# A block triangular inverse on TensorE: 64 by 64 products for 128 by 128 ones, and two weight-split steps at other places

## The reference

```
a_mat = where(strict, (k_beta @ k.T) * decay, 0)
sol   = triangular_solve(a_mat + I, rhs, lower=True, unit_diagonal=True)
u, w  = sol[..., :dv], sol[..., dv:]
```

## Time and profile before

| | us |
|---|---|
| median of 3 runs | 945.17 |
| the profiled execution | 945.2 |
| its span in the trace | 943.3 |
| TensorE matmuls busy | 921.9 (98%) |
| VectorE busy | 610.8 (65%) |
| ScalarE busy | 497.4 (53%) |
| GpSimd busy | 31.1 (3%) |

### The profile page before, as it was taken

The page is one execution under the profiler, slowest core; times in us unless marked ns, Lnnn a source line. Parts: engine busy times, 40 slices in busy tenths (PEclk is TensorE's granted clock), DMA queues, the critical chain, the costliest instruction groups (busy, mean ns, idle before and its releaser), DMA issues.

```text
span 943.3 us, 13998 instructions
## 1 busy us (share of the span) xinstructions
PE 921.9 (98%) x5274; PEld 784.3 (83%) x5274; DVE 610.8 (65%) x1039; ACT 497.4 (53%) x868; POOL 31.1 (3%) x43
## 2 busy tenths in 40 slices
PE   8999989999999999899999999999999999999998
PEld 6999889799989898767888888888876788888887
DVE  6787966776565687778655555556887665555443
ACT  5478441473565566566544444545576654444432
POOL 2001000000000012100000000010000000000000
PEclk9999999999999999999999999999999999999999
DMA  9545231366444545214555655555434365555560
GB/s 331 180 135 159 92 97 46 122 210 212 149 134 136 183 154 192 90 45 134 179 178 180 192 190 191 182 181 180 142 128 133 92 197 192 188 178 178 180 200 22
DMA packets 106293, 148.22 MB, mean 157 GB/s; under 512 B 12564, under 2 KB 59344, under 8 KB 106112
## 3 DMA queue, kind: packets, MB, share of 16 engines
q1 hardware_dynamic: 102014, 145.34, 47.5%
q0 software_dynamic: 704, 1.77, 0.5%
q10 hardware_dynamic: 3522, 0.39, 0.3%
HBM read 146.03 MB, written 1.45 MB: 156 GB/s over the span
## 4 chain that ended last, share of the span: by engine, by line
PE 87%; DVE 7%; ACT 4%; issue 1%; DMA 1%; ACTq 0%; SPq 0%; DVEq 0%
PE ps L1889 25%; PE ps L1891 25%; PE ps L1890 24%; PE ps L1989 4%; DVE wlo L1162 3%; ACT whi L642 1%; PE ps L2135 1%; PE ps L2129 1%; DMA raw<-in_a_w_in 1%; PE ps L2283 1%; DVE G L1334 1%; PE ps L2491 0%; PE ps L2522 0%; PE ps L2070 0%; PE ps L2089 0%
## 5 line engine op out<-in xcount | busy, mean ns | idle before, releaser
L1162 DVE TENSOR_TENSOR wlo<-raw,whi 128x1024 fp32r<-128x1024 f32 (+1 forms) x271 | 320.3, 1223 | 210.9 <-ACT whi L642 210.6
L642 ACT ACTIVATE whi<-raw 128x1024 fp32r<-128x1024 f32 (+1 forms) x271 | 270.2, 1045 | 269.1 <-PE ps L1891 269.0
L1889 PE MATMUL ps<-whi,xh 128*128 128x512 f32 (+1 forms) x544 | 217.8, 400 | 0.9 <-DVE wlo L1162 0.6
L1891 PE MATMUL ps<-whi,xl 128*128 128x512 f32 (+1 forms) x544 | 211.7, 389 | 0.0
L1890 PE MATMUL ps<-wlo,xh 128*128 128x512 f32 (+1 forms) x544 | 211.6, 389 | 0.0
L1889 PEld LDWEIGHTS ps<-whi,xh 128*128 128x128 f32 x544 | 102.2, 188 | 22.5 <-issue 2.6
L1891 PEld LDWEIGHTS ps<-whi,xl 128*128 128x128 f32 x544 | 102.1, 188 | 21.6
L1890 PEld LDWEIGHTS ps<-wlo,xh 128*128 128x128 f32 x544 | 102.4, 188 | 18.5
L1889 PE MATMUL ps<-xh,whi 128*128 128x256 f32 x384 | 111.4, 290 | 1.1 <-DVE xl L1228 0.7
L1891 PE MATMUL ps<-xh,wlo 128*128 128x256 f32 x384 | 108.6, 283 | 0.0
L1890 PE MATMUL ps<-xl,whi 128*128 128x256 f32 x384 | 108.6, 283 | 0.0
(11 more groups left out here) (400 smaller groups left out, 1185.3 us busy)
## 6 DMA issues: line engine op xcount, KB each, us to landing
raw<-in_l_w_gate SPq DMA_DIRECT2D x44, 512.0 KB, 3.8
raw<-in_l_w_up SPq DMA_DIRECT2D x44, 512.0 KB, 4.7
raw<-in_l_w_down SPq DMA_DIRECT2D x44, 512.0 KB, 4.6
raw<-in_l_w_in SPq DMA_DIRECT2D x36, 512.0 KB, 4.4
raw<-in_a_w_in SPq DMA_DIRECT2D x32, 512.0 KB, 4.6
raw<-in_w_kv SPq DMA_DIRECT2D x16, 512.0 KB, 4.7
raw<-in_b_w_in SPq DMA_DIRECT2D x16, 512.0 KB, 4.5
raw<-in_l_w_o SPq DMA_DIRECT2D x16, 512.0 KB, 4.6
```

The lines of the kernel that those rows point to most:

```text
L642: nc.scalar.activation(whi[:, g % HIGH, a], raw[:, g % RAW, a], ACT.Copy).then_inc(hi_done, 1)
L1162: nc.vector.tensor_tensor(wlo[:, g % LOW, a], raw[:, g % RAW, a], whi[:, g % HIGH, a].bitcast(F32), ALU.subtract).then_inc(lo_done, 1)
L1889: mm(o_, a_h, b_h, start=start, stop=False, skip_group_check=True)
L1891: return mm(o_, a_l, b_h, start=False, stop=stop, skip_group_check=True)
```

## The change

Only the triangular inverse and its two neighbours are touched:

- **Products.** In levels 0 and 1 each 128 by 128 product becomes two of 64 by 64, the upper left and the lower right diagonal block (`HALVES`). They use array rows 0 to 63 with columns 0 to 63, and rows 64 to 127 with columns 64 to 127, and write 64 columns of the same PSUM bank, in partitions 0 to 63 and 64 to 127. In level 2 there is only one of 64 by 64: for step 1 rows 64 to 127 into columns 0 to 63, for step 3 rows 0 to 63 into columns 0 to 63.
- **VectorE.** The masked step reads 128 by 256 in place of 128 by 512 for each group; in level 2 it is a plain copy of 64 by 256. The subtraction is two operations of 64 by 256 for each group in levels 0 and 1 (one for each half of the partitions, so `inv` counts twice as many), and in level 2 one multiplication by -1 of 64 by 256 that writes the upper right block, which was zero.
- **Masks.** The two masks that are left are stored 64 wide. The columns of the third stay unused.
- **Low parts.** The low part of `U_Z+2` moves from behind level 0 to between groups 1 and 2 of its masked step. That of `U_Z+3` moves from behind level 1 to behind level 2.

The transposes (step 5) and ScalarE's copies stay as they were.

```diff
@@ -64,7 +64,8 @@
     c[:, MNEG:MNEG + P] = np.where(r <= f, 0.0, NEG)
     for n, s in enumerate(LEVELS):
         m = (r // (2 * s) == f // (2 * s)) & ((r // s) % 2 == 0) & ((f // s) % 2 == 1)
-        c[:, LMT + n * P:LMT + (n + 1) * P] = m
+        if n < 2:
+            c[:, LMT + n * 64:LMT + (n + 1) * 64] = np.where(r < 64, m[:, 0:64], m[:, 64:P])
     diagonal = np.where(f <= r, 0.0, NEG)
     c[:, CAUSAL:CAUSAL + P] = diagonal
     c[:, CAUSAL + 2 * P:CAUSAL + 3 * P] = diagonal
@@ -235,6 +236,7 @@
 
         half = lambda t, h: t[64 * (h % 2):64 * (h % 2) + 64]
         SPAN = (slice(0, P), slice(P, 3 * P))
+        HALVES = (slice(0, 64), slice(64, P))
 
         conv_col = lambda w, m: cols[:, 0, w * CONV_T + m:w * CONV_T + m + 1]
         r0 = CONV_W * CONV_T
@@ -1449,19 +1451,29 @@
 
             for lv in range(3):
                 for q_ in range(4):
-                    a = slice(512 * q_, 512 * q_ + 512)
+                    to, by = G[:, 4, 256 * q_:256 * q_ + 256], ps[:, 4 + q_, 0:256]
+                    if lv == 0 and q_ == 2:
+                        lo_until(U_Z + 3)
                     dve.wait_ge(S("t2"), 4 * lv + q_ + 1)
                     if lv == 0:
                         dve.wait_ge(S("kk_d"), 8)
-                    nc.vector.tensor_tensor(quad(G[:, 4, a]), quad(ps[:, 4 + q_, :]), over4(LMT + lv * P), ALU.mult)\
-                        .then_inc(S("t2m"), 1)
+                    if lv < 2:
+                        mask = C[:, LMT + 64 * lv:LMT + 64 * lv + 64].unsqueeze(1).to_broadcast([P, 4, 64])
+                        nc.vector.tensor_tensor(quad(to), quad(by), mask, ALU.mult).then_inc(S("t2m"), 1)
+                    else:
+                        nc.vector.tensor_copy(to[0:64], by[0:64]).then_inc(S("t2m"), 1)
                 for q_ in range(4):
-                    a = slice(512 * q_, 512 * q_ + 512)
+                    four = lambda r, c: quad(Y[r, 512 * q_:512 * q_ + 512])[:, :, c]
+                    by = quad(ps[:, 4 + q_, 0:256])
                     dve.wait_ge(S("blocks"), 32 * NB + 32)
                     dve.wait_ge(S("p1"), 4 * lv + q_ + 1)
-                    nc.vector.tensor_tensor(Y[:, a], Y[:, a], ps[:, 4 + q_, :], ALU.subtract).then_inc(S("inv"), 1)
-                if lv < 2:
-                    lo_until(U_Z + 3 + lv)
+                    if lv < 2:
+                        for b in HALVES:
+                            nc.vector.tensor_tensor(four(b, b), four(b, b), by[b], ALU.subtract).then_inc(S("inv"), 1)
+                    else:
+                        nc.vector.tensor_scalar(four(HALVES[0], HALVES[1]), by[HALVES[0]], -1.0, None, ALU.mult)\
+                            .then_inc(S("inv"), 1)
+            lo_until(U_Z + 4)
 
             v4, o4 = by_head(G[:, 2, :]), by_head(G[:, 4, :])
             zs = G[:, 3, :].rearrange("p (t h d) -> p t h d", t=NT, h=HEADS)
@@ -2125,17 +2137,21 @@
                         pe.wait_ge(S("vb"), 4 * q_ + 4)
                     else:
                         pe.wait_ge(S("inv_x"), 4 * lv - 4 + q_ + 1)
+                    up, low_ = HALVES
                     for n, a in enumerate(tiles(q_)):
-                        last = mm(ps[:, 4 + q_, P * n:P * n + P], G[:, 8, a], Y[:, a], start=True, stop=True)
+                        for to, by in (((up, up), (low_, low_)) if lv < 2 else ((up, low_),)):
+                            last = mm(ps[to, 4 + q_, 64 * n:64 * n + 64], G[by, 8, a][:, to], Y[by, a][:, by], start=True, stop=True)
                     last.then_inc(S("t2"), 1)
                 for q_ in range(4):
                     pe.wait_ge(S("t2m"), 4 * lv + q_ + 1)
                     pe.wait_ge(S("x_blocks"), 16 * NB + 16)
                     for n, a in enumerate(tiles(q_)):
-                        last = mm(ps[:, 4 + q_, P * n:P * n + P], G[:, 10, a], G[:, 4, a], start=True, stop=True)
+                        for b in HALVES if lv < 2 else HALVES[:1]:
+                            last = mm(ps[b, 4 + q_, 64 * n:64 * n + 64], G[b, 10, a][:, b],
+                                      G[b, 4, 256 * q_ + 64 * n:256 * q_ + 64 * n + 64], start=True, stop=True)
                     last.then_inc(S("p1"), 1)
                 for q_ in range(4 if lv < 2 else 0):
-                    pe.wait_ge(S("inv"), 4 * lv + q_ + 1)
+                    pe.wait_ge(S("inv"), 8 * lv + 2 * q_ + 2)
                     turn(S("turned"), 4 + q_, [Y[:, a] for a in tiles(q_)])
             pe.wait_ge(acc_read["A"], 1)
             pe.wait_ge(*past("q", "root", 1))
@@ -2143,7 +2159,7 @@
                                                                   G[:, 9, :], G[:, 6, :]))
             part = lambda b, h: ps[:, b + h // 4, P * (h % 4):P * (h % 4) + P]
             for h in range(HEADS):
-                pe.wait_ge(S("inv"), 8 + h // 2 + 1)
+                pe.wait_ge(S("inv"), 16 + h // 2 + 1)
                 last = mm(part(0, h), y4[:, h, 0, :], v4[:, h, 0, :], start=True, stop=True)
                 if h % 4 == 3:
                     last.then_inc(S("u_ps"), 1)
```

## The result

The changed kernel takes **940.32 us** (median of 5 executions, 939.52 to 940.54) beside 945.09 us of the kernel before on the same chip (5 executions, 945.07 to 946.6). The ratio is 0.994, with a 95% interval of 0.9928 to 0.9951. It is faster by 4.8 us, where 8.0 was forecast. The profiled execution took 940.32 us too; the one of before took 945.2.

What follows compares the result with a forecast made beforehand. TensorE's own work was taken to bound the levels of the inverse. Gains of 1.7, 2.9 and 3.4 us in levels 0, 1 and 2 gave 8.0: 945.2 - 8.0 = 937.2 us, range 936.0 to 942.6 (8 in 10).

Steps and rivals of the forecast that it cites:

- The forecast's own range: Whole kernel: 936.0 us (no shape cost, subtractions fully behind the products) to 938.8 (0.85 and 0.1 both doubled).
- Rival 1: Levels 0 and 1: no pairs in one PSUM bank, 64 matmuls take 3.57 us; 942.1 us; chance 0.12.
- Rival 2: Levels 0 and 1: small tiles' loads and products overlap badly, batch 2.4 to 3.0 us; 939 to 941; chance 0.13.
- Pairs, and streaming of 56 ns: Levels 0 and 1: 64 matmuls of 56 ns, two at once, make a batch 1.79 us, before 3.57.
- rival 3: Levels' products: a floor under each matmul; no gain at 67 ns, 957 us at 112; chances 0.07 same, 0.05 slower.
- Level 2: Last level's two product batches: 3.58 + 0.1 us, before 7.15; gain 3.4, `u` starts at 139.6.
- The start of the subtractions, and what follows them: Levels 0 and 1: first subtraction 0.85 us after step 3 starts; behind the last, 0.05 + 0.45 + 0.1 us.
- The subtractions: VectorE in levels 0 and 1: eight of 256 elements in a row take 7 x 0.34 + 0.42 = 2.8 us.
- The clock: TensorE in the levels: taken at 2.4 GHz; a granted clock below 1.00 listed as a sign of error.
- The moved low parts: VectorE, `U_Z+2` in level 0, `U_Z+3` behind level 2: cost nothing; some 1 us saved that the sum never counts.
- Rival 4: Behind the levels: gain given back by weights or VectorE's low parts, within 1.9 us of no change; chance 0.03.
- no cost for the shapes: TensorE in the levels: leaves out the 0.1 us for each change between full array and parts, four on the path.

Runs made afterwards that it cites:

- e3: Changed kernel with each group's four upper blocks issued first, then its four lower ones: 942.38 us, ratio 0.9965 to the kernel before.
- e9: Changed kernel with the subtractions of levels 0 and 1 ordered upper, lower, lower, upper, and so on: 939.78 us, ratio 0.9928 to the kernel before.
- e7: Changed kernel with the subtractions of all upper halves first, then all lower ones, in levels 0 and 1: 940.34 us, ratio 0.9940 to the kernel before.
- e4: Changed kernel with four subtractions of 64 by 512, each over two groups, in place of eight: 941.12 us, ratio 0.9949 to the kernel before.
- e6: Changed kernel plus 12 constant 128 by 128 products on TensorE, five ahead of level 0, seven behind its groups 0 and 1: 940.04 us, ratio 0.9935.
- e11: Changed kernel plus only the seven constant products behind groups 0 and 1 of level 0, none ahead: 939.55 us, ratio 0.9928 to the kernel before.
- e8: Kernel before with only the two low parts moved, products still 128 by 128: 946.43 us, ratio 1.0001 to the kernel before.
- e10: Changed kernel plus the 12 constant products of e6 and the subtraction order of e9: 940.87 us, ratio 0.9933 to the kernel before.
- e12: Changed kernel plus the seven constant products of e11 and the subtraction order of e9: 939.76 us, ratio 0.9927 to the kernel before.
- e2: Changed kernel with the two low parts put back behind levels 0 and 1: 941.37 us, ratio 0.9951 to the kernel before.

## Why the prediction was right, and where its sum was off

The forecast's gain was 8.0 us, the measured one 4.8, inside the range of 936.0 to 942.6 but outside the forecast's own 936.0 to 938.8. So that the range held is in part luck: it had been widened for rivals 1 and 2, and neither came; what came were two costs that no case had priced. `u` started at 142.71 where 139.6 stood, 3.1 us late. Point by point:

- **Pairs, and streaming of 56 ns: right.** A batch takes 1.91 us where 1.79 stood. Rival 1 (no pairs in one bank, 3.57) and rival 3 (a floor under each matmul of 60 ns and more) are refuted: 30 ns for each matmul held through 64 in a row, and 58 ns through 32 where there are no pairs. The Trainium skill ("TensorEngine Tiling (Array Packing)", "Restrictions and Gotchas") says that different row tiles can't access one PSUM bank at once; these pairs did, and the measurement decides for pairs like these, which write different partitions of the bank. No run here has two row halves that write the same partitions of one bank at once. The Trainium skill ("TensorE: Matmul & The Clock Gate", "What happens when you issue a matmul") gives about 62 ns for each matmul where it is decoded in microcode; that did not show either. Rival 2's duration, 2.4 to 3.0 us, came only when the blocks stood apart (e3).
- **Level 2: right.** 3.69 us for 3.7.
- **The start of the subtractions, and what follows them: right.** In level 1, they start 2.66 us into the level (1.79 + 0.85 = 2.64 stood), and the next level starts 0.65 us behind their end (0.6).
- **The subtractions: the term that was mis-sized.** "Two of these take 0.76 us, so a further one adds 0.34": the rows it rests on the earlier trace rows are operations on all 128 partitions. The new ones take turns between the two halves, and a further one adds 0.45. So eight take 3.56 instead of 2.77, 0.8 us more in each of levels 0 and 1, **1.6 us**. e9 and e7 show the 0.34 where the half stays the same; e4 shows 0.71 for two turns of twice the size.
- **The clock: the assumption that failed.** The sum took every duration at 2.4 GHz and named a lower clock only as a sign of error. With half the products TensorE has more idle time in level 0, and there its clock fell in both profiled executions of the changed kernel; the mean clock of each of its 10 executions is below 1.000. That the idle time is the cause is borne out by the fills, which kept the clock at 1.000 in 9 of the 10 executions of e6 and e11, but not shown to be all of it, as e8, e10 and e12 had falls there too. Price: **1.24 us** by e11 (1.28 by e6). It comes between the start of `V`'s transposes and the first subtraction: 122.47 to 127.93 is 5.46 us, and in e11 122.50 to 126.69 is 4.19.
- **The rest** of the 3.1 us is 0.3. Group 3 of step 1 is 0.2 of it: in e11 it starts at 125.42 where 125.23 stood.
- **The moved low parts: right.** Hidden in both places, by a hair in the second, as said. The copy of `state` starts 3.10 us behind `u` (142.71 to 145.81), and in e2, which has no low part there, 3.10 too (143.86 to 146.96). e2 measures the saving of "some 1 us that the sum never counts" at 1.0 us; e8 measures it at nothing without the new products. So the moves are part of the gain of the products.
- **Nothing is given back:** 795.7 us from `u` to the end in both. Rival 4 did not come.
- **The forecast's own range: not what its words give.** With 0.85 doubled in two levels and 0.1 in four places it ends at 937.2 + 1.7 + 0.4 = 939.3, not 938.8. With no cost for the shapes, and the last subtraction one operation behind the products (0.85 + 2.77 - 1.79 - 0.42 = 1.4 us less a level), it starts near 934, not at 936.0. The measured time lies above it either way.
- **Two small slips:** the 16-column row gives 0.12 us by its own difference, where 112 ns were used (rival 3 would be 959, not 957), and eight matmuls of 512 columns, four at once, stream for 0.89 us at 111.6 ns for 128 columns, not 0.85. Neither moves the sum.

So 8.0 - 1.6 - 1.24 - 0.2 = 4.96 us, and 4.91 was measured at `u` (4.88 in the time of the profiled executions, 945.2 - 940.32).

Two things stay open. Why products ahead of level 0 make two DMA issues take twice as long was not tried further. Nor was it settled why the clock falls in some executions, in level 0 or at 722 us, and not in others of the same program; the kernel before has executions below 1.000 too, but their trace was not taken.

## What to carry to other kernels

Where only diagonal blocks of a product are wanted, give TensorE the blocks in row and column halves of the array, and issue the two halves as neighbours: here the batch took half its time. Then cost the engine that becomes the bound at its new shape, which half of the partitions it works on included. And when an edit halves TensorE's work at a place where it also waits, look at the granted clock there before adding up durations at the full one.

## What the runs showed of the hardware that had not been expected

- **VectorE and partition halves.** Operations of 64 by 256, each 0.42 us, start 0.34 us apart if they stay in one half of the partitions, and 0.45 apart if they change it. At 64 by 512, with a change each time, they start 0.71 apart.
- **TensorE finds partners that are not neighbours**, at a price: 2.46 us for a batch, between 1.91 and 3.57. By the rows of e3, matmuls in different halves of the array don't all start in the order of the program.
- **The clock fell in level 0 and in one place far behind it**, in some executions of a program and not in others (at 722 us in the traces of e9, e10 and e12), behind stretches in which TensorE was partly idle (busy 2.89 of 5.50 us from 118.5 us in the changed kernel, 1.36 of 3.00 from 718 us in e12). Being partly idle doesn't always bring it: with 3.38 of 5.50 the kernel before kept its clock. In level 0 the fall began at 120.5 us in one trace and at 124.4 in another, and lasted 3.4, 6.8 or 10.2 us. With small products of constants in level 0 it stayed at 1.000 in all 5 executions of e6, in 4 of 5 of e11, and in 2 of 5 each of e10 and e12. Executions of the kernel before differ by some 1.6 us with it.
- **DMA issues of 1.9 us for two in place of 0.96**, on SP and on ScalarE, when TensorE had products of constants ahead of level 0.
